# An S5 mixer's batch loop on one core: lag products placed right behind the additions, and the reading and turning tables stored with real and imaginary parts apart

## What is computed

```
lam_bar = exp(lam * dt)                       # complex, (groups, state)
b_bar   = ((lam_bar - 1) / lam) * B           # (groups, state, 16)
bu      = einsum('blgp,gnp->blgn', u, b_bar)
x_t     = lam_bar * x_{t-1} + bu_t            # scan over 528 positions
y       = real(einsum('blgn,gpn->blgp', x, C)) + D * u
g       = gelu(y);   out = (g @ w_glu_a) * sigmoid(g @ w_glu_b)
```

## Time and profile before

| | |
|---|---|
| times of three runs | 1195.01, 1200.85, 1202.56 us; median 1200.85 us |
| the profiled execution | 1203.49 us, its span 1201.5 us, mean granted clock of PE 0.99 |
| PE busy | 1143.7 us (95%) |
| DVE, ACT, POOL busy | 554.2 us (46%), 410.3 us (34%), 185.7 us (15%) |
| PE busy by fortieths of the span, the first seven | 4, 3, 9, 9, 9, 9, 9 tenths |
| POOL busy, the first seven | 2, 9, 7, 8, 5, 0, 0 tenths |

### The profile page before, as it was taken

How to read it: one execution, slowest core, us unless ns; L and a number is a source line. 1 busy time by engine, 2 the same in 40 slices (tenths; PEclk the granted TensorE clock), 3 DMA queues, 4 the chain that set the end, 5 groups by cost and what they waited for, 6 DMA issues and landing times.

```text
span 1201.5 us, 20385 instructions
## 1 busy us (share of the span) xinstructions
PE 1143.7 (95%) x8339; PEld 1027.6 (86%) x8339; DVE 554.2 (46%) x821; ACT 410.3 (34%) x698; POOL 185.7 (15%) x137
## 2 busy tenths in 40 slices
PE   4399999999999999999999989989999999999997
PEld 4388899999999999999999866668888888888886
DVE  5778734444433343334444355555434343434443
ACT  5723232323222222223333355543323222223332
POOL 2978500002111111100000000000212111110000
PEclk9999989999999999999999999999999999999999
DMA  7225441323232232223223311113322333223332
GB/s 130 79 56 110 105 124 54 106 71 106 70 105 81 94 99 75 87 71 96 75 91 106 123 37 37 36 40 101 105 88 87 105 105 96 78 75 96 97 96 90
DMA packets 119385, 104.61 MB, mean 87 GB/s; under 512 B 21868, under 2 KB 117216, under 8 KB 119008
## 3 DMA queue, kind: packets, MB, share of 16 engines
q1 hardware_dynamic: 110120, 99.85, 27.9%
q10 hardware_dynamic: 9216, 4.06, 1.4%
HBM read 98.11 MB, written 5.24 MB: 86 GB/s over the span
## 4 chain that ended last, share of the span: by engine, by line
issue 44%; PE 43%; DVE 4%; DMA 3%; SPq 2%; POOL 2%; ACT 1%; ACTq 0%; POOLq 0%; DVEq 0%
PE banks L1314 39%; POOL gate L574 2%; SPq L387 1%; DMA k_toep<-k_dram 1%; PE banks L1436 1%; PE banks L1426 1%; DMA raw_c_re<-in_ssm_c_re 1%; DMA k_dram<-k_lag 1%; PE banks L1375 1%; PE banks L1376 1%; ACT u_row L631 1%; DMA y_feat<-y_dram 0%; PE banks L1410 0%; PE banks L1339 0%; DVE pow_t L995 0%
## 5 line engine op out<-in xcount | busy, mean ns | idle before, releaser
L596 ACT CAST w_high<-raw 128x1024 fp32r<-128x1024 f32 x186 | 195.0, 1049 | 573.2 <-PE banks L1314 573.1
L910 DVE TENSOR_TENSOR w_low<-raw,w_high 128x1024 fp32r<-128x1024 f32 x186 | 228.3, 1228 | 208.3 <-ACT w_high L596 208.3
L1314 PE MATMUL banks<-x_high,w_high 128*128 128x512 f32 (+2 forms) x1184 | 320.7, 324 | 1.0 <-DVE x_low L1128 1.0
L1314 PE MATMUL banks<-x_high,w_low 128*128 128x512 f32 (+2 forms) x1184 | 318.3, 322 | 0.0
L1314 PE MATMUL banks<-x_low,w_high 128*128 128x512 f32 (+2 forms) x1184 | 317.5, 321 | 0.0
L1314 PEld LDWEIGHTS banks<-x_high,w_high 128*128 128x128 f32 x1184 | 198.8, 189 | 19.4 <-issue 2.2
L1314 PEld LDWEIGHTS banks<-x_high,w_low 128*128 128x128 f32 x1184 | 198.1, 188 | 16.7
L1314 PEld LDWEIGHTS banks<-x_low,w_high 128*128 128x128 f32 x1184 | 198.7, 188 | 15.9
L1314 PE MATMUL banks<-a_high,w_high 128*128 128x256 f32 (+2 forms) x528 | 140.3, 320 | 0.0
L1314 PE MATMUL banks<-a_high,w_low 128*128 128x256 f32 (+2 forms) x528 | 140.2, 320 | 0.0
L1314 PE MATMUL banks<-a_low,w_high 128*128 128x256 f32 (+2 forms) x528 | 140.2, 320 | 0.0
(11 more groups left out here) (278 smaller groups left out, 1261.7 us busy)
## 6 DMA issues: line engine op xcount, KB each, us to landing
raw<-in_ffn_w_gate SPq DMA_DIRECT2D x22, 1024.0 KB, 5.2
raw<-in_ffn_w_up SPq DMA_DIRECT2D x22, 1024.0 KB, 5.3
raw<-in_ffn_w_down SPq DMA_DIRECT2D x16, 768.0 KB, 4.5
raw<-in_ffn_w_down SPq DMA_DIRECT2D x16, 640.0 KB, 4.4
raw<-in_attn_w_qkv SPq DMA_DIRECT2D x6, 1024.0 KB, 5.0
raw<-in_ssm_w_glu_b SPq DMA_DIRECT2D x4, 1024.0 KB, 5.7
raw<-in_ssm_w_glu_a SPq DMA_DIRECT2D x4, 1024.0 KB, 5.8
k_toep<-k_dram SPq DMA_DIRECT2D x64, 64.0 KB, 2.6
```

The source lines that it names most:

```text
L596: nc.scalar.copy(high[:, j], raw[:, slot, :, j * P:(j + 1) * P]).then_inc(w_rounded, 1)
L910: nc.vector.tensor_tensor(low[:, j], raw[:, slot, :, j * P:(j + 1) * P], high[:, j], ALU.subtract).then_inc(w_split, 1)
L1314: ins = nc.tensor.matmul(banks[:, bank + h, b0:b0 + cn], w[:, j, k, :], xx[:, first_k + k, c0 + base:c0 + base + cn], start=start and k == ...
```

## The change

Four things are changed. The tables `read` and `turn` have their real and imaginary planes outermost, where before the two stood side by side in each pair; so `reads` and `turns` become six instructions on half the elements each (four products, a sum and a difference) in place of three. The tables in pair layout that fed the old form (`c_cross`, `power_re`, `power_im`, `fine_pair`, `fine_cross`, `coarse_pair`) and the copies that made them are gone; `powr`, `fine` and `coarse` are read directly, and one-element memsets (two behind the powers, one behind `fine`) carry the signals. PE's loop has lags(b + 1) right behind additions(b + 1), and injection(b + 2) alternates with the outputs from the first pair on. Behind the loop, the GLU's early products go one by one behind each pair's outputs of batch 6.

```diff
-        fine_cross = sb("fine_cross", [P, PAIRS, 2, TA], scope=early)
-        coarse_pair = sb("coarse_pair", [P, 2, PAIRS, 2, TA], scope=early)
-        c_pair = sb("c_pair", [P, PAIRS, 2, GROUP], scope=s5)
-        c_cross = sb("c_cross", [P, PAIRS, 2, GROUP], scope=s5)
-        power_re = sb("power_re", [P, PAIRS, 2, T], scope=s5)
-        power_im = sb("power_im", [P, PAIRS, 2, T], scope=s5)
-        fine_pair = sb("fine_pair", [P, PAIRS, 2, TA], scope=s5)
...
-        read = sb("read", [P, 3, PB, 2, T + 1, GROUP], scope=s5)
-        read_t = sb("read_t", [P, PB, 2, T, GROUP], scope=s5)
+        read = sb("read", [P, 3, 2, PB, T + 1, GROUP], scope=s5)
+        read_t = sb("read_t", [P, PB, T, GROUP], scope=s5)
-        turn = sb("turn", [P, 2, PB, 2, CS], scope=s5)
-        turn_t = sb("turn_t", [P, PB, 2, TA, TA], scope=s5)
+        turn = sb("turn", [P, 2, 2, PB, CS], scope=s5)
+        turn_t = sb("turn_t", [P, 2, PB, TA, TA], scope=s5)
@@ turns(b), POOL
-                nc.gpsimd.tensor_tensor(grid.rearrange("p n (a f) -> p n a f", f=TA), g_re, f, ALU.mult)
-                step(nc.gpsimd.tensor_tensor(cross, g_im, f_cross, ALU.mult))
-                nc.gpsimd.tensor_tensor(grid, grid, cross.rearrange("p n a f -> p n (a f)"), ALU.add).then_inc(turn_ready, 1)
+                shape = [P, PB, TA, TA]
+                fr, fi = (fine[:, i, pr, 0:TA].unsqueeze(2).to_broadcast(shape) for i in range(2))
+                gr, gi = (coarse[:, i, pr, 0:TA].unsqueeze(3).to_broadcast(shape) for i in range(2))
+                tr, ti = (turn[:, b % 2, i, :, 0:TA * TA].rearrange("p r (a f) -> p r a f", f=TA) for i in range(2))
+                nc.gpsimd.tensor_tensor(tr, gr, fr, ALU.mult)
+                nc.gpsimd.tensor_tensor(turn_t[:, 0], gi, fi, ALU.mult)
+                nc.gpsimd.tensor_tensor(ti, gr, fi, ALU.mult)
+                step(nc.gpsimd.tensor_tensor(turn_t[:, 1], gi, fr, ALU.mult))
+                nc.gpsimd.tensor_tensor(tr, tr, turn_t[:, 0], ALU.subtract)
+                nc.gpsimd.tensor_tensor(ti, ti, turn_t[:, 1], ALU.add).then_inc(turn_ready, 1)
@@ reads(b), POOL
-                nc.gpsimd.tensor_tensor(table, c, l_re, ALU.mult)
-                step(nc.gpsimd.tensor_tensor(cross, c_x, l_im, ALU.mult))
-                nc.gpsimd.tensor_tensor(flat_table, flat_table, cross.rearrange("p n t q -> p n (t q)"), ALU.add).then_inc(read_ready, 1)
+                rr, ri = read[:, b % 3, 0], read[:, b % 3, 1]
+                cr = nat["c_re"][:, pr, :].unsqueeze(2)
+                ci = nat["neg_c_im"][:, pr, :].unsqueeze(2)
+                shape = [P, PB, T, GROUP]
+                lr = powr[:, 0, 1:T + 1, pr].rearrange("p t r -> p r t").unsqueeze(3).to_broadcast(shape)
+                li = powr[:, 1, 1:T + 1, pr].rearrange("p t r -> p r t").unsqueeze(3).to_broadcast(shape)
+                crb, cib = cr.to_broadcast(shape), ci.to_broadcast(shape)
+                nc.gpsimd.tensor_tensor(rr[:, :, 1:, :], crb, lr, ALU.mult)
+                step(nc.gpsimd.tensor_tensor(read_t[:], cib, li, ALU.mult))
+                nc.gpsimd.tensor_tensor(rr[:, :, 1:, :], rr[:, :, 1:, :], read_t[:], ALU.add)
+                step(nc.gpsimd.tensor_tensor(ri[:, :, 1:, :], cib, lr, ALU.mult))
+                step(nc.gpsimd.tensor_tensor(read_t[:], crb, li, ALU.mult))
+                nc.gpsimd.tensor_tensor(ri[:, :, 1:, :], ri[:, :, 1:, :], read_t[:], ALU.subtract).then_inc(read_ready, 1)
@@ POOL, ahead of reads(0) and of turns(0)
-            nc.gpsimd.tensor_copy(c_cross[:, :, 0], c_pair[:, :, 1])
-            step(nc.gpsimd.tensor_copy(c_cross[:, :, 1], c_pair[:, :, 0]))
-            nc.gpsimd.tensor_copy(coarse_pair[:, 0], coarse[:, 0, :, 0:TA].unsqueeze(2).to_broadcast([P, PAIRS, 2, TA]))
-            step(nc.gpsimd.tensor_copy(coarse_pair[:, 1], coarse[:, 1, :, 0:TA].unsqueeze(2).to_broadcast([P, PAIRS, 2, TA])))
@@ read_starts(b), ACT
-                nc.scalar.copy(read[:, b % 3].rearrange("p r i t q -> p (r i) t q")[:, :, 0, :],
-                               c_pair[:, pr].rearrange("p r i q -> p (r i) q")).then_inc(starts_ready, 1)
+                nc.scalar.copy(read[:, b % 3, 0, :, 0, :], nat["c_re"][:, pr, :])
+                nc.scalar.copy(read[:, b % 3, 1, :, 0, :], nat["neg_c_im"][:, pr, :]).then_inc(starts_ready, 1)
@@ DVE, behind the powers and behind fine
-            nc.vector.tensor_copy(power_re[:], by_pair[:, 0].unsqueeze(2).to_broadcast([P, PAIRS, 2, T]))
-            nc.vector.tensor_copy(power_im[:, :, 0], by_pair[:, 1])
-            TS(power_im[:, :, 1], by_pair[:, 1], -1.0, None, ALU.mult).then_inc(powers_ready, 1)
+            step(nc.vector.memset(pow_t[:, 0, 0, 0:1], 0.0))
+            nc.vector.memset(pow_t[:, 0, 0, 0:1], 0.0).then_inc(powers_ready, 1)
-            nc.vector.tensor_copy(fine_pair[:], fine[:, :, :, 0:TA].rearrange("p i r f -> p r i f"))
-            TS(fine_cross[:, :, 0], fine[:, 1, :, 0:TA], -1.0, None, ALU.mult)
-            nc.vector.tensor_copy(fine_cross[:, :, 1], fine[:, 0, :, 0:TA]).then_inc(fine_ready, 1)
+            nc.vector.memset(pow_t[:, 0, 0, 0:1], 0.0).then_inc(fine_ready, 1)
@@ DVE, the state of a batch (the same again behind the scan)
-                TT(zt[:], v4, ti, ALU.mult)
-                step(TT(v4, v4, tr, ALU.mult))
+                TT(cross, v, ti, ALU.mult)
+                step(TT(v, v, tr, ALU.mult))
@@ DVE, behind the last batch
-            dve.wait_ge(read_ready, BATCHES)
@@ PE, the loop over b
                 additions(b + 1)
-                outputs(b, 0)
                 if b >= 1:
                     lags(b + 1)
-                injection(b + 2, 0, 1)
+                injection(b + 2, 0)
+                within_chunks(b, 0)
+                injection(b + 2, 1)
+                read_outs(b, 0)
+                injection(b + 2, 2)
                 within_chunks(b, 1)
-                injection(b + 2, 2)
+                injection(b + 2, 3)
                 read_outs(b, 1)
-                injection(b + 2, 3)
+                injection(b + 2, 4)
                 within_chunks(b, 2)
-                injection(b + 2, 4, 5)
+                injection(b + 2, 5)
                 read_outs(b, 2)
                 injection(b + 2, 6, 7)
                 outputs(b, 3)
             lags(BATCHES - 1)
             additions(BATCHES - 1)
-            outputs(BATCHES - 2, 0, 1)
-            early_glu(0, 0, 2)
-            outputs(BATCHES - 2, 2, 3)
-            early_glu(0, 2, 3)
+            for r_ in range(PB):
+                outputs(BATCHES - 2, r_)
+                early_glu(0, r_, r_ + 1)
             outputs(BATCHES - 1, 0, 1)
-            early_glu(0, 3, 4)
+            early_glu(0, 4, 5)
             outputs(BATCHES - 1, 2, 3)
-            early_glu(0, 4, GLU_EARLY)
+            early_glu(0, 5, GLU_EARLY)
             early_glu(1, 0, GLU_EARLY)
```

More of the change, by code:

```diff
@@ L207, in trunk @@
         u_state = sb("u_state", [P, GROUPS, C], scope=s5)
-        nat = {k: sb("nat_" + k, [P, PAIRS, GROUP], scope=s5) for k in ("b_re", "b_im")}
-        c_pair = sb("c_pair", [P, PAIRS, 2, GROUP], scope=s5)
-        c_cross = sb("c_cross", [P, PAIRS, 2, GROUP], scope=s5)
-        power_re = sb("power_re", [P, PAIRS, 2, T], scope=s5)
-        power_im = sb("power_im", [P, PAIRS, 2, T], scope=s5)
-        fine_pair = sb("fine_pair", [P, PAIRS, 2, TA], scope=s5)
+        nat = {k: sb("nat_" + k, [P, PAIRS, GROUP], scope=s5) for k in ("b_re", "b_im", "c_re", "neg_c_im")}
         bbar_pair = sb("bbar_pair", [P, 2, PAIRS, 2 * GROUP], scope=s5)
         lam_t = sb("lam_t", [P, len(LAM_NAMES), PAIRS], scope=s5)
+        powr = sb("powr", [P, 2, T + 1, PAIRS], scope=s5)
+        fine = sb("fine", [P, 2, PAIRS, TA + 1], scope=s5)
         coarse = sb("coarse", [P, 2, PAIRS, TA + 1], scope=s5)
+        pow_t = sb("pow_t", [P, 2, 4, PAIRS], scope=s5)
         s5.close()
@@ L663, in side @@
                 nc.scalar.copy(decay_row[:, b % 2, :, 1:], lam_t[:, 4, pr].unsqueeze(2).to_broadcast([P, PB, CS - 1]))
-                nc.scalar.copy(turn[:, b % 2, :, :, TA * TA], coarse[:, :, pr, TA].rearrange("p i r -> p r i")).then_inc(side_ready, 1)
+                nc.scalar.copy(turn[:, b % 2, :, :, TA * TA], coarse[:, :, pr, TA]).then_inc(side_ready, 1)
             def read_starts(b):
@@ L1083, in _ @@
                 pr = slice(b * PB, (b + 1) * PB)
-                tr, ti = (turn[:, b % 2, :, i].unsqueeze(1).to_broadcast([P, 2, PB, CS]) for i in range(2))
+                tr, ti = (flat(turn[:, b % 2, i]).unsqueeze(1).to_broadcast([P, 2, PB * CS]) for i in range(2))
                 v, cross, out = state_banks(), zt[:].rearrange("p i r c -> p i (r c)"), state[:, b % 2].rearrange("p i r c -> p i (r c)")
-                v4 = v.rearrange("p i (r c) -> p i r c", c=CS)
                 dve.wait_ge(turn_ready, b + 1)
@@ L1410, in lags @@
                         ins = nc.tensor.matmul(lag_rows(r_), bbar_pair[:, i, b * PB + r_, :],
```

(4 more changed lines are left out.)

22 lines of the change are left out of this document (2 added, 20 removed).

## The result

The changed kernel took **1209.51 us** (median of 20 executions, 1200.14 to 1213.66) against 1201.95 us for the kernel before (20 executions beside it, 1195.01 to 1205.74). The ratio is 1.0048, interval 1.0025 to 1.0072: slower by about half a per cent, where 1195.5 had been forecast, with 1189 to 1203 as the range. Two executions of the kernel before, of 2251 and 2843 us beside r1 to r4, are left aside in all that follows.

A forecast was written before the change was run, and what follows sets the result against it. PE was taken as the bound, its mixer waits the only gain. Reads(7) earlier (-4.4 us) and the clock behind the loop (-1.4) gave -5.8: 1197.7 against the profiled 1203.49, 1195.1 against the median; forecast 1195.5, range 1189 to 1203.

The forecast's parts named there:

- Part A: Ahead of the loop: removed copies and an earlier reads(0) make b_bar 2.7 us early, bounds 1.2 and 3.8.
- upper bound of 3.8 us: Ahead of the loop: b_bar's gain if halved POOL instructions let DVE's table work run free.
- The prices of POOL's instructions: Tables: products 0.64 us on 256 elements, 1.07 on 512; sums 0.65 and 1.19; a pair 10.6 to 10.7 us.
- The reads are last: 136.9 in place of 141.27: Loop's end: six POOL pairs at 10.9 us end reads(7) at 136.9, gaining 4.4 us, the start's 2.7 included.
- part C: Behind the loop: worth nothing at the old clock, 2.9 us if the low clock goes; half, 1.4, was taken.
- Waits of about the same size elsewhere in the loop left the clock high: Behind the loop: reason for taking only half of the 2.9 us clock gain, 1.4.
- Rival 3: PE stands at injection tables, lags or the last split, with a longer low clock; at most 1 us stays: 1200, chance 0.20.
- the 1.0 us wait for `inj_t`: Loop's first iteration, sign of being right: PE waits 1.0 us for the injection table, additions ending 75.3, table 76.28.
- long run's start within 164 to 167: Behind the mixer, sign of being right: PE's long run of products starts at 164 to 167, before at 171.61.
- a pair of over 11.6 us: Loop, sign of being wrong: POOL's turns and reads together take over 11.6 us, where 10.9 was forecast.
- a wait of over 2 us at L1410: PE's lags, sign of being wrong: a wait over 2 us, where about 0.5 for `read` was forecast.
- Rival 1: Loop: POOL's tables become the bound, products at a sum's rate, a pair 12.5 us; time 1207, chance 0.12.

The follow-up runs named there:

- r1: The changed kernel again, with no edit: 1201.35 us, ratio 1.0034 to the kernel before.
- r4: The changed kernel with the last additions put ahead of the last lags: 1209.52 us, ratio 1.0071 to the kernel before.
- r3: The kernel before with the new tables only, PE's order left as it was: 1202.75 us, ratio 1.0005.
- r10: The changed kernel with DVE's first split of GLU weights made to wait for the last reads: 1203.51 us, ratio 1.0017 to the kernel before.
- r11: The kernel before with PE's new order, old tables, and the first product of reads(7) done twice: 1200.11 us, ratio 1.0010.
- r2: The kernel before with PE's new order only, tables, copies and waits as they were: 1197.71 us, ratio 0.9982.
- r7: The changed kernel without the imaginary plane of the last reading table, so part of the computation is missing: 1199.07 us, ratio 0.9971 to the kernel before.
- r5: The changed kernel with 24 unused identity products in front of the last lags: 1206.87 us, ratio 1.0033 to the kernel before.
- r6: The kernel before with PE's new order, old tables, and the first product of reads(7) done three times: 1211.26 us, ratio 1.0076.
- r12: The kernel before with PE's new order except in the first iteration, reads(0) in six from `powr`, pair-table copies on ACT: 1194.29 us, ratio 0.9944.

## Why the prediction was wrong

**Part A held in kind; 2.0 of 2.7 us came.** Reads(0) run from 31.38 to 38.62 (forecast 31.7 to 38.5). B_bar is done at 45.35 (forecast 44.6, before 47.3). In between seven of DVE's twelve table instructions from 30.0 to 39.5 us take 1.0 to 1.6 us, beside POOL's; four rows of the timeline of DVE:

```profile
34.90 1.14 DVE L991 TENSOR_TENSOR fine<-fine,pow_t 128x64 f32<-128x64 f32 x1
36.08 1.20 DVE L986 TENSOR_TENSOR fine<-fine 128x128 f32<-128x128 f32 x1
37.21 0.28 DVE L987 TENSOR_TENSOR pow_t<-fine 128x128 f32<-128x128 f32 x1
37.41 1.37 DVE L988 TENSOR_TENSOR fine<-fine 128x128 f32<-128x128 f32 x1
```

Each is held up for less than before, but more of them are, and the table ends only with reads(0): the halves let nothing run free, so the upper bound of 3.8 us was not reached. The table ended at 39.50 in place of 40.83, so 1.3 us early where 1.95 had been put; that is what part A lacks. The loop's turns(2) start at 71.73 (forecast 71.45).

**The prices of POOL's instructions held; the pair didn't.** Products take 0.65 us on 256 elements and 1.10 on 512, sums 0.68 and 1.27: reading `powr` at a stride costs nothing that shows (each value read serves 16 elements in a row, so this says nothing of a stride at every element). But the small excess of each adds up to 10.88 us for a pair that nothing holds up, where 10.6 had been put: 6 x 0.28 = 1.7 us. From the third pair on one instruction is held up beside DVE (11.36 us a pair, 0.47 more), and in the last one more by the split of weights, 0.98: 4 x 0.47 + 0.98 = 2.9 us, where 6 x 0.3 = 1.8 had been put. The 0.98 comes of the timing alone: DVE reached the split 2.9 us earlier than before (134.20 against 137.14) and POOL ended its reads 4.0 us later. The prediction costed DVE's split of `glu` beside POOL, and not this one. The wait for `read_ready` that the diff takes out stands behind it and has no part in it. With the start 0.3 us late, 0.3 + 1.7 + 1.1 puts the end of reads(7) at 139.91 in place of 136.9.

**The step that failed** is "The reads are last: 136.9 in place of 141.27", with what part C made of the clock behind it. POOL's pair was put at 10.9 us and took 11.36 on average, so the reads ended at 139.91; PE came at 137.1 and stood 2.88 us, where a wait of about 0.5 had been put. Part C then priced the clock as something that could only come back ("so I take half, 1.4"). The sentence "Waits of about the same size elsewhere in the loop left the clock high" was true of the profile before, and no ground for this place. The runs showed a cost instead: behind a wait of 1.6 to 2.9 us 29 of 68 executions are in the low group, and the three of them that were profiled (r3, r10, r11) had about 27 us at the lower level. Rival 3 had the mechanism, a low clock in a longer stretch behind a stand at the lags, and 1200 as its price. The low executions of the changed kernel take 1209 to 1214.

**And the base was a low one.** The profile before has a granted clock of 0.53 over 3.6 us and of 0.52 over 10.5 us; 3.6 x 0.47 + 10.5 x 0.48 = 6.7 us of full speed. So 171.61 less 6.7 is 164.9. After has 166.70 less the 0.34 x 5 = 1.7 of its own window, 165.0. This is an estimate, as part of a low stretch can be hidden; by it the change gains nothing at full clock, and the 4.9 us of the profiled pair are clock. The executions go with it: of the 98 of before 30 have a mean clock of 0.993 or more and a median of 1196.8, 61 have 0.986 to 0.990 and 1203.4; the nine better ones of after, 1200.1 to 1202.2, are slower than nearly all of the 30. That the gap of 6.6 us is this stretch of the mixer is not shown: r2 and r7, whose profiles have 1.00 from 130 to 170 us, have two such groups as well, 5 to 6 us apart (0.993 or more, and 0.988). The forecast took 1.7 us of it in its -4.4 as a gain of the tables.

**Right were** the end of the five waits for the blocks, the 1.0 us wait for `inj_t` in the first iteration, now measured to the digit, and that the time stays within 1% of before. The long run's start within 164 to 167 is luck in part: at the last lags only 1.3 us of the 4.4 were gained (141.27 to 139.97), and 3.6 behind them, where 1.4 had been put; 3.3 of these are clock (10.5 x 0.48 = 5.0 in before, less 1.7). A sign of failure was a pair of over 11.6 us; the average stayed under it, and only the last pair, 12.34, went over. The listed sign of failure, "a wait of over 2 us at L1410" (L1396 after), is what came. Outputs(7) are done at 156.96, a little outside the 153 to 156. Rival 1 did not come: the lags were not later than before, and its rule, a sum's rate for products too, did not hold (products on 512 elements take 1.10 us, sums 1.27).

**Why the parts don't add up**: the order makes PE earlier at the last lags, the tables make POOL later there: reads(7) end at 135.95 in before, at 137.07 with the order alone and at 139.91 with both. Alone the first leaves no wait (0.998) and the second 2.0 us (1.0005); together it is 2.9 us (1.0048, and 1.0034 in r1).

**Still open**: what decides, in one execution, whether a wait of 1.6 to 2.9 us is followed by the low stretch; and why r5's executions spread over 10 us without it (their clocks are 0.987 to 0.997). Other places than the mixer take part in such spreads: 240 to 260 us was granted 0.91 in r1 and 1.00 in after, the same kernel. No run held everything else equal and moved the wait in small steps.

## What to carry to other kernels

Before a change is priced from a profile, compare its mean granted clock with those of the other runs: gains that are only a low stretch not repeated are not the change's. A change that lets the matrix engine arrive earlier at a point that another engine does not reach earlier makes an idle gap, and the gap can cost several times its length; so look where the last wait of a phase will stand, cost what each engine will newly run beside when one gets earlier and another later, and if the gap can't be closed, try filling it. Splitting an instruction in two lets others pass between, but where they share a port it also gives them more places to hold it up.

## What the runs showed of the hardware

- In the profiled low executions a wait of 1.6 to 3.7 us of PE (in r4 two, 1.8 and 1.0) was followed by about 27 us at the 1.2 GHz level (r3, r4, r10, r11) or 34 (r6), an estimate from the clocks of the 5 us windows. PE was busy 5.00 of 5.00 us in each window at 0.50, but for 4.68 in the first of r6. By the mean clocks of all executions it was so every time at 3.7 us (6 of 6), and 29 of 68 times at 1.6 to 2.9 us. The same program on the same input gives both.
- Shorter waits were followed by shorter low stretches. In the profile before, two waits of 0.93 us stand in front of the 3.6 us at 0.53 and the 10.5 us at 0.52; other waits of this size had none behind them.

```profile
130.34 0.66 PE L1426 MATMUL banks<-u_state,k_toep 128*128 128x66 f32 x4 [0.93 <-DMA k_toep<-k_dram]
...
151.43 0.66 PE L1426 MATMUL banks<-u_state,k_toep 128*128 128x66 f32 x4 [0.93 <-DMA k_toep<-k_dram]
```

- The low stretches farther back vary too: 680 to 700 and 780 to 800 us were granted 0.91 and 0.91 before, 0.83 and 0.83 after, with no instruction there changed. From the start of the long run to the end it was 1029.9 us in before and 1029.8 in r12 (0.91 and 0.92), but 1031.9 in after.
- A product of two broadcast operands on POOL costs nearly the same when one is read at a stride of 32 elements, each value 16 times in a row (1.10 us, 512 elements), as when both are dense tables (1.07).
